# Order of the front: a weight block between row tiles of x, x turned by pairs, the bias row first

## The reference, cut to what matters

```
h = rmsnorm(x, g_mix)                      # x * rsqrt(mean(x*x) + EPS) * gain
proj = h @ w_in                            # 1024 x 6656
q, k, v, u, gate_a, gate_s = split(proj)   # u is 512 wide, the input of the SSM
attn = diff_attention(q, k, v, rel_bias[t5_bucket(rel)], ...)
y    = s5_ssm(u, ...)                      # parameters prepared from a_re, a_im, dt, b, c
mixed = sigmoid(gate_a)*attn + sigmoid(gate_s)*glu(gelu(y) @ w_glu)
x = x + mixed @ w_out;  x = x + relu(rmsnorm(x) @ w1)**2 @ w2;  return rmsnorm(x)
```

## Time and profile before

| | |
|---|---|
| median of 3 runs | 764.02 us (763.57 to 764.18) |
| profiled execution, its own time | 763.78 us |
| its span on the core | 762.0 us |
| PE busy | 745.2 us (98%), 3754 matmuls |
| DVE, ACT, POOL busy | 530.5, 359.2, 28.3 us |
| DMA | 85.21 MB, mean 112 GB/s |

### The profile page before, as it was taken

How to read it: one execution, slowest core, us unless ns; L and a number is a source line. 1 busy time by engine, 2 the same in 40 slices (tenths; PEclk the granted TensorE clock), 3 DMA queues, 4 the chain that set the end, 5 groups by cost and what they waited for, 6 DMA issues and landing times.

```text
span 762.0 us, 10030 instructions
## 1 busy us (share of the span) xinstructions
PE 745.2 (98%) x3754; PEld 608.7 (80%) x3754; DVE 530.5 (70%) x953; ACT 359.2 (47%) x630; POOL 28.3 (4%) x27
## 2 busy tenths in 40 slices
PE   5999999999999999999999999999999999999996
PEld 4878888777777777888888888788888888888885
DVE  4679999665556673436743578866886498748897
ACT  7524631265556663732322645434543345335455
POOL 3210000000000100000000000000000000000015
PEclk9999999999999999999999999999999999999998
DMA  7773439932224430237237130282108320742002
GB/s 246 203 163 116 103 110 163 209 93 71 70 70 122 155 111 3 87 106 248 83 111 194 57 109 29 65 225 98 56 1 235 124 84 0 186 146 83 28 1 111
DMA packets 91824, 85.21 MB, mean 112 GB/s; under 512 B 10028, under 2 KB 68064, under 8 KB 91776
## 3 DMA queue, kind: packets, MB, share of 16 engines
q1 hardware_dynamic: 90944, 82.85, 39.0%
q10 hardware_dynamic: 832, 1.71, 1.1%
HBM read 77.11 MB, written 5.34 MB: 108 GB/s over the span
## 4 chain that ended last, share of the span: by engine, by line
PE 90%; DVE 4%; ACT 3%; issue 2%; DMA 1%; POOL 0%; SPq 0%; DVEq 0%; ACTq 0%
PE ps L1651 27%; PE ps L1653 26%; PE ps L1652 26%; PE ps L1941 3%; PE ps L1922 2%; PE ps L1931 1%; DMA mixA<-in_x 1%; DVE w_lo L1414 1%; PE ps L1726 1%; DVE fr L1427 1%; ACT fa_hi L884 1%; PE ps L1855 1%; ACT w_hi L615 1%; PE ps L1838 1%; PE ps L1815 0%
## 5 line engine op out<-in xcount | busy, mean ns | idle before, releaser
L1651 PE MATMUL ps<-hT_hi,w_hi 128*128 128x512 f32 x384 | 152.5, 397 | 0.5 <-DVE hT_lo L983 0.3
L1653 PE MATMUL ps<-hT_hi,w_lo 128*128 128x512 f32 x384 | 149.9, 390 | 0.0
L1652 PE MATMUL ps<-hT_lo,w_hi 128*128 128x512 f32 x384 | 149.6, 390 | 0.0
L1651 PE MATMUL ps<-w_hi,hT_hi 128*128 128x512 f32 x288 | 113.9, 395 | 1.1 <-POOL w_lo L557 1.1
L1653 PE MATMUL ps<-w_hi,hT_lo 128*128 128x512 f32 x288 | 112.3, 390 | 0.0
L1652 PE MATMUL ps<-w_lo,hT_hi 128*128 128x512 f32 x288 | 112.1, 389 | 0.0
L851 ACT ACTIVATE w_hi<-raw 128x1024 fp32r<-128x1024 f32 x78 | 81.7, 1053 | 56.4 <-PE ps L1653 56.4
L1414 DVE TENSOR_TENSOR w_lo<-raw,w_hi 128x1024 fp32r<-128x1024 f32 x78 | 94.1, 1219 | 16.0 <-ACT w_hi L851 15.0
L615 ACT ACTIVATE w_hi<-raw 128x1024 fp32r<-128x1024 f32 x62 | 64.7, 1057 | 56.7 <-PE ps L1653 51.0
L1011 DVE TENSOR_TENSOR w_lo<-raw,w_hi 128x1024 fp32r<-128x1024 f32 x58 | 70.0, 1220 | 29.5 <-ACT w_hi L615 28.9
L1651 PE MATMUL ps<-w_hi,fa_hi 128*128 128x512 f32 x224 | 87.4, 390 | 1.0 <-DVE w_lo L1414 1.0
(11 more groups left out here) (258 smaller groups left out, 998.0 us busy)
## 6 DMA issues: line engine op xcount, KB each, us to landing
raw<-in_w SPq DMA_DIRECT2D x64, 512.0 KB, 4.2
raw<-in_w_in SPq DMA_DIRECT2D x44, 512.0 KB, 5.3
raw<-in_w_glu SPq DMA_DIRECT2D x8, 512.0 KB, 3.9
raw<-in_w_out SPq DMA_DIRECT2D x8, 512.0 KB, 3.9
mixA<-in_x SPq DMA_DIRECT2D x4, 512.0 KB, 5.1
bias<-frow_dram SPq DMA_DIRECT2D x32, 64.0 KB, 2.0
toep<-taps_dram SPq DMA_DIRECT2D x8, 256.0 KB, 12.5
x<-in_x SPq DMA_DIRECT2D x4, 512.0 KB, 6.7
```

The source lines that it names most:

```text
L1651: nc.tensor.matmul(dst, a_hi, b_hi, start=start, stop=False)
L1652: nc.tensor.matmul(dst, a_hi, b_lo, start=False, stop=False)
L1653: return nc.tensor.matmul(dst, a_lo, b_hi, start=False, stop=stop)
```

## The change

Three things are reordered; the arithmetic stays.

1. SP issues x tiles 0 and 1, unit 0, x tiles 2 and 3, units 1 to 3. `rb` and `oneh` move from SP's list to ACT's queue, behind the three gain columns, with a semaphore of their own (`onehot_in`).
2. x is turned and split by pairs. A pair g is the blocks k = 2g, 2g+1 of row tiles 0 and 1 (256 columns each); the "late" part is the same blocks of row tiles 2 and 3. For k = 0, 1 row tiles 2 and 3 are handled one by one (128 columns). The transposes stand partly between the products. `w_lo` of unit 0 is made by DVE in two halves; POOL makes units 1 to 3.
3. The two bias row matmuls are PE's first instructions, behind `onehot_in`; DVE's copies of `frow` stand between its scalings of row tiles 2 and 3.

```diff
 # SP
-        for u in range(RING):
+        load_x(0)
+        load_x(1)
+        load_raw(0)
+        load_x(2)
+        load_x(3)
+        for u in range(1, RING):
             load_raw(u)
...
-                         (rel_bias, rb[:, :]), (onehot, oneh[:, :]),
 # POOL
-        for u in range(U_V):
+        pool.wait_ge(w_lo_done, 1)
+        for u in range(1, U_V):
 # ACT
+        act.dma_start(rb[:, :], rel_bias).then_inc(onehot_in, 16)
+        act.dma_start(oneh[:, :], onehot).then_inc(onehot_in, 16)
...
+        x_stats(0)
+        x_stats(1)
         act.wait_ge(cols_turned, 1)
-        nc.scalar.activation(cols[:, :], ps[:, turn_bank(0, KT - 1), 0:2 * KT + UT],
-                             ACT.Identity).then_inc(cols_copied, 1)
+        nc.scalar.activation(cols[:, :], ps[:, 5, 0:2 * KT + UT], ACT.Identity).then_inc(cols_copied, 1)
...
+        def x_hi(k, t0, t1, done):
+            nc.scalar.activation(hT_hi[:, k, P * t0:P * t1], x_turned(k, t0, t1), ACT.Identity,
+                                 scale=g1_col[:, k:k + 1]).then_inc(done, 1)
+        def hi_pair(g):
+            act.wait_ge(pair_turned, g + 1)
+            for k in (2 * g, 2 * g + 1):
+                x_hi(k, 0, 2, pair_hi)
+        def hi_late(g):
+            act.wait_ge(turned, 2 * g + 2)
+            for k in (2 * g, 2 * g + 1):
+                x_hi(k, 2, 4, hT_hi_done)
         split_hi(0)
         act.wait_ge(cols_copied, 1)
-        for k in range(KT):
-            turn_hi(0, k, g1_col)
-            if k == 2:
-                split_hi(1)
+        hi_pair(0)
+        x_stats(2)
+        x_stats(3)
+        act.wait_ge(third_turned, 1)
+        for k in range(2):
+            x_hi(k, 2, 3, third_hi)
+        split_hi(1)
+        act.wait_ge(turned, 2)
+        for k in range(2):
+            x_hi(k, 3, 4, hT_hi_done)
+        hi_pair(1)
+        hi_late(1)
+        hi_pair(2)
+        hi_pair(3)
         for u in range(U_SSM, U_V):
             split_hi(u + 2)
             if u == 0:
+                hi_late(2)
+                hi_late(3)
                 act.wait_ge(prm_in, 16 * N_PRM)
 # DVE (x_lo, lo_pair, lo_late are the counterparts of x_hi, hi_pair, hi_late)
+        scale_x(0)
+        scale_x(1)
+        dve.wait_ge(w_hi_done, 1)
         dve.wait_ge(cols_copied, 1)
-        for k in range(KT):
-            turn_lo(0, k, g1_col)
+        TT(w_lo[:, 0, 0:512], raw[:, 0, 0:512], w_hi[:, 0, 0:512].bitcast(F32), ALU.subtract).then_inc(w0_part, 1)
+        lo_pair(0)
+        TT(w_lo[:, 0, 512:], raw[:, 0, 512:], w_hi[:, 0, 512:].bitcast(F32), ALU.subtract).then_inc(w_lo_done, 1)
+        scale_x(2)
+        dve.wait_ge(frow_mm, 1)
+        TS(frow[:, 0:512], ps[0:N_HEADS, 7, :], 1.0, None, ALU.mult).then_inc(frow_out, 1)
+        TS(frow[:, 512:BIAS_W], ps[0:N_HEADS, 6, 0:BIAS_W - 512], 0.0, MASKED, ALU.mult, ALU.add).then_inc(frow_out, 1)
+        scale_x(3)
+        dve.wait_ge(third_hi, 2)
+        for k in range(2):
+            x_lo(k, 2, 3, third_lo)
+        dve.wait_ge(hT_hi_done, 2)
+        for k in range(2):
+            x_lo(k, 3, 4, hT_lo_done)
+        lo_pair(1)
+        lo_late(1)
+        lo_pair(2)
+        lo_pair(3)
+        lo_late(2)
+        lo_late(3)
 # PE
+        pe.wait_ge(onehot_in, 32)
+        nc.tensor.matmul(ps[0:N_HEADS, 7, :], rb[:, :], oneh[:, 0:512], start=True, stop=True)
+        nc.tensor.matmul(ps[0:N_HEADS, 6, 0:BIAS_W - 512], rb[:, :], oneh[:, 512:BIAS_W], start=True,
+                         stop=True).then_inc(frow_mm, 1)
         pe.wait_ge(ident_set, 2)
+        pe.wait_ge(cols_in, 16 * N_COLS)
+        nc.tensor.transpose(ps[:, 5, 0:2 * KT + UT], cols_nat[:, :],
+                            ident[0:2 * KT + UT, 0:2 * KT + UT]).then_inc(cols_turned, 1)
+        pe.wait_ge(x_scaled, 1)
+        for k in range(4):
+            turn_x(0, k)
+        pe.wait_ge(x_scaled, 2)
+        for k in range(4):
+            mm = turn_x(1, k)
+            if k % 2:
+                mm.then_inc(pair_turned, 1)
+        def first_waits(t):
+            if t == 0:
+                pe.wait_ge(w0_part, 1)
+                pe.wait_ge(pair_lo, 1)
+            elif t == 1:
+                pe.wait_ge(cols_copied, 1)
+            elif t == 2:
+                pe.wait_ge(frow_out, 2)
+                pe.wait_ge(third_lo, 2)
+            else:
+                pe.wait_ge(hT_lo_done, 2)
         for u in range(U_SSM, U_V):
-            pe.wait_ge(w_lo_done, u + 1)
+            if u:
+                pe.wait_ge(w_lo_done, u + 1)
+                pe.wait_ge(pair_lo, 2 * u + 2)
             for t in range(TOK):
...
                 for k in (2 * u, 2 * u + 1):
+                    if u == U_SSM and t == 0 and k == 1:
+                        pe.wait_ge(w_lo_done, 1)
+                        pe.wait_ge(pair_lo, 2)
...
+                if u == U_SSM and t == 1:
+                    for t3 in range(2, TOK):
+                        pe.wait_ge(x_scaled, t3 + 1)
+                        for k3 in range(2):
+                            mm = turn_x(t3, k3)
+                        if t3 == 2:
+                            mm.then_inc(third_turned, 1)
+                        else:
+                            mm.then_inc(turned, 2)
+            if u == U_SSM:
+                turn_x_late(1)
+                turn_x_pair(2)
+                turn_x_pair(3)
+            if u == U_SSM + 1:
+                turn_x_late(2)
+                turn_x_late(3)
...
             row_unit_mm(u, (u - U_V) // 4, (u - U_V) % 4, 4, hT_hi, hT_lo, None, 0)
             if u == U_V:
                 turn_prm()
-                bias_row()
```

More of the change, by code:

```diff
@@ L214, in build @@
     c12_joined = sem("c12_joined"); p7_joined = sem("p7_joined"); c22_joined = sem("c22_joined"); c21_joined = sem("c21_joined")
-    consts_in = sem("consts_in"); prm_in = sem("prm_in"); gfin_in = sem("gfin_in")
+    consts_in = sem("consts_in"); onehot_in = sem("onehot_in"); w0_part = sem("w0_part"); prm_in = sem("prm_in"); gfin_in = sem("gfin_in")
     frow_out = sem("frow_out"); frow_done = sem("frow_done"); frow_mm = sem("frow_mm")
@@ L224, in build @@
     scale_ready = sem("scale_ready"); x_rt = sem("x_rt"); x_rstd = sem("x_rstd"); x_scaled = sem("x_scaled")
+    pair_turned = sem("pair_turned"); pair_hi = sem("pair_hi"); pair_lo = sem("pair_lo")
+    third_turned = sem("third_turned"); third_hi = sem("third_hi"); third_lo = sem("third_lo")
     turned = sem("turned"); hT_hi_done = sem("hT_hi_done"); hT_lo_done = sem("hT_lo_done")
@@ L378, in turn_bank, with x_place, x_turned @@
             return k - 4
-        return (B_T + k) % 8 if g == 0 else B_T + k % 4
+        return B_T + k % 4
+    def x_place(t, k):
+        c0 = 256 * (k % 2) + P * (t % 2)
+        bank = (2 if t == 2 else 3) if t >= 2 and k < 2 else ((0, 1, 2, 3), (None, 0, 1, 0))[t // 2][k // 2]
+        return bank, c0
+    def x_turned(k, t0, t1):
+        bank, c0 = x_place(t0, k)
+        return ps[:, bank, c0:c0 + P * (t1 - t0)]
     def wait_rows(eng, c, t):
@@ L390, in _, with load_x @@
     def _(sp):
-        for t in range(TOK):
+        def load_x(t):
             sp.dma_start(mixA[:, t, :], x[0, P * t:P * t + P, :]).then_inc(x_in[t], 16)
@@ L597, in _, with x_stats @@
             act.dma_start(dst, src).then_inc(cols_in, 16)
-        for t in range(TOK):
+        act.dma_start(rb[:, :], rel_bias).then_inc(onehot_in, 16)
+        act.dma_start(oneh[:, :], onehot).then_inc(onehot_in, 16)
+        def x_stats(t):
             act.wait_ge(x_in[t], 16)
@@ L985, in turn_lo, with scale_x @@
             ins.then_inc(hT_lo_done, 1)
-        for t in range(TOK):
+        def scale_x(t):
             dve.wait_ge(x_rt, t + 1)
@@ L992, in _, with x_lo, lo_pair, lo_late @@
             TS(mixA[:, t, :], mixA[:, t, :], rstd[:, 0, t:t + 1], None, ALU.mult).then_inc(x_scaled, 1)
-        dve.wait_ge(cols_copied, 1)
-        for k in range(KT):
-            turn_lo(0, k, g1_col)
+        def x_lo(k, t0, t1, done):
+            tc_ = slice(P * t0, P * t1)
+            STT(out=hT_lo[:, k, tc_], in0=x_turned(k, t0, t1), scalar=g1_col[:, k:k + 1],
+                in1=hT_hi[:, k, tc_].bitcast(F32), op0=ALU.mult, op1=ALU.subtract).then_inc(done, 1)
+        def lo_pair(g):
+            dve.wait_ge(pair_hi, 2 * g + 2)
+            for k in (2 * g, 2 * g + 1):
+                x_lo(k, 0, 2, pair_lo)
+        def lo_late(g):
+            dve.wait_ge(hT_hi_done, 2 * g + 2)
+            for k in (2 * g, 2 * g + 1):
+                x_lo(k, 2, 4, hT_lo_done)
+        scale_x(0)
+        scale_x(1)
+        dve.wait_ge(w_hi_done, 1)
+        dve.wait_ge(cols_copied, 1)
+        TT(w_lo[:, 0, 0:512], raw[:, 0, 0:512], w_hi[:, 0, 0:512].bitcast(F32), ALU.subtract).then_inc(w0_part, 1)
[18 more added lines that the diff above has]
+        lo_late(3)
         def prow(i):
@@ L1730, in turn_x @@
         def turn_x(t, k):
-            return nc.tensor.transpose(ps[:, turn_bank(0, k), P * t:P * t + P], mixA[:, t, P * k:P * k + P],
```

(18 more changed lines are left out.)

17 lines of the change are left out of this document (8 added, 9 removed).

## The result

| | before | after |
|---|---|---|
| median of the runs | 764.1 us (763.57 to 767.92) | 781.56 us (780.62 to 782.6) |
| ratio | | 1.0223 (1.0212 to 1.0234) |
| profiled execution | 763.78 us | 782.6 us |
| its span | 762.0 us | 780.8 us |

The change makes the kernel 17.5 us slower, against a forecast of 6.3 with an upper bound of 8.2. The sign was right and the size far out.

The account below looks back on a forecast made before the run. PE's matmul stream, busy 98% of the span, was taken as the bound, its shift carried to the end. 2.8 + 1.3 + 0.9 + 2.5 - 1.2 = +6.3 on 764.0 gave 770.3 us, range 766.0 to 772.2.

Parts of the forecast that it names:

- Steps 1 and 2: Front: one-hot table lands at 9.6 us, bias row takes 2.2, first product starts at 14.7 against 14.17.
- Step 3: Unit 0: waits on DVE and ACT before row tiles 2 and 3 end it at 22.5, not 19.74: +2.8 us.
- Steps 4 to 6: Transposes inside the stream +1.3 and +0.9, hole before unit 3 +2.5, bias row leaving after unit 4 -1.2 us.
- step 5: Unit 3: its split waits behind ACT's list, so PE has a hole; +2.5 us, bounds 2.3 and 3.2.
- The last paragraph: Signs to check in the trace, among them unit 4 starting near 43.4 and PE idling 2.3 to 3.2 before unit 3.
- the clock falls in the hole: Rival: PE's clock drops in the hole before unit 3, some 3.7 us at half speed lose 1.8: 772.1; chance 0.10.
- nothing behind it waits for a fixed time: Behind unit 4: every microsecond its start moves is carried unchanged to the end.
- nothing more is late: Behind the hole before unit 3: splits and low parts of later units still come in time, no further loss.
- at nothing: Changes counted as free: SP's order, its shorter list, POOL without unit 0, later frees of the raw ring.
- step 7: SP's reordered loads, its shorter list, POOL's lost unit 0 and later raw ring frees add no further time.
- step 6: Behind unit 4: the bias row leaves the stream, -1.2 us; DVE loses frow copies that PE did not wait for.
- The other side: Rival at the front: oneh lands by 5, first product at 9.8, unit 0 ends at 15.7: 763.5; chance 0.13.

Follow-up runs that it names:

- the exponentials first: Changed kernel, ACT making the exponentials and unit 3's split before the late parts of pairs 2 and 3, DVE's late parts also later: 778.19 us, ratio 1.0176.
- the bias row back: Changed kernel with the bias row matmuls and DVE's frow copies behind unit 4 again, rb and oneh staying on ACT's queue: 771.33 us, ratio 1.0083.
- matmuls through the gap: Changed kernel with bias row and ACT order edits, warm-up and row tile 2 turned early, plus 12 fp32 matmuls behind the first pair's turning: 764.5 us.
- held store: Changed kernel with one more ACT wait, putting the frow store 0.4 us behind the last load of u: 782.2 us, ratio 1.0184.
- DVE's wait: Changed kernel with the frow store held behind the loads of u, and DVE's large products waiting for GpSimd's copy: 774.21 us, ratio 1.013.
- the late store: Changed kernel with ACT's store of the bias rows moved to one unit behind the turning of u: 771.75 us, ratio 1.0128.

## Why the prediction was right in sign and wrong in size

- **Steps 1 and 2 held.** The table landed at 9.0 (9.6; the range was made for 9.0 to 10.7), the bias row took 2.2, the first product came at 14.64 (14.7). ACT's wait for the turned columns was 4.7 us, as said.
- **Step 3 was mis-sized**, +4.9 and not +2.8. I priced the products of unit 0 at 0.23 each, and twelve of them took 0.43. I had noted that the clock goes from 1.2 to 2.4 GHz at 10.3 in the kernel before, and took that as a time of day. It is none: it rose at 4.93 where PE worked from 1.5 on, at 20.0 in the kernel after, whose PE starts at 9.05 and not 6.67 and is idle in between, and once at 14.92 behind the same transposes as before. With the clock the order of waits changed too. I had DVE as the last before row tile 2, at 18.9; it was free at 18.0 and waited 3.0 us more for the transposes, which PE reached at 19.9. The wait before row tile 3 did not come.
- **Steps 4 to 6 held.** Transposes inside the stream, the hole of 2.2 and 0.3 of lost overlap before unit 3 (+2.5), the bias row (-1.15). L1025's counterpart took 0.28 us, as step 5 assumed. (The last paragraph has unit 4 near 43.4; its own terms give 43.6.) The run with the exponentials first shows that the hole is made by ACT's order.
- **The rival "the clock falls in the hole" happened** in the profiled run, with the price it had (1.7 for 1.8), and I gave it 0.10. I had argued from a fall 2.6 us after the last matmul of the program that a hole of 2.5 was just too short; the hole was 2.2, and the fall came all the same. It is a matter of the run: the six times of the kernel after lie in two groups, 780.62 to 780.82 and 782.29 to 782.6, 1.7 apart, which is what one such fall costs. The trace is of the second group; that the first ran without the fall is not shown.
- **Where it failed: "nothing behind it waits for a fixed time", and with it "nothing more is late" in step 5 and "at nothing" in step 7.** I took a stream without a hole up to unit 4 to be one that carries a shift unchanged to the end. It has a second chain beside it, from u through memory and GpSimd back to PE, and that one was not shifted but reordered. In step 6 I saw that DVE is rid of the `frow` copies and that PE did not wait for them; I did not ask who else waited. ACT did, with the store of 640 KB, and its wait was what kept the store behind the loads of u. Then the copy missed its place ahead of DVE's products. It cost 8.7 of the 12.5 us by which the forecast was short of the profiled run; late clock in unit 0 and clock behind the hole are the rest (2.1 and 1.7). The store is not the whole of it: with the store behind the loads, but the clock down behind the hole, the time was 782.2. The shift of u against DVE's block (13.0 against 7.8 us), which I had taken for one and the same, is enough for the same 8.7.
- The other side, an early front, stayed out because of the table, as argued. But the run with the bias row back shows that it would not have won even so: with the exponentials first as well and first products at 10.5 to 11.4, three of the four kernels end 1.4 to 3.5 us behind the old one (764.57 in the runs beside them), and the one with matmuls through the gap is level with it (764.5, ratio 0.9999 to 1.0016).

## What to carry to other kernels

When an operation moves to an earlier place, follow everything that waited for its result, the DMAs first: a wait that costs nothing may be what keeps a large store behind a load that matters. A shift of the main stream may be added up only as far as the next place where a second chain (memory, another engine) joins it, and each such place has to be looked up with its slack on both sides. Price matmuls behind a changed start at both clock levels, and count a hole like the one of 2.2 us here as a hole plus a possible 1.7 us of slow matmuls. Before a difference of a microsecond or two between medians is put down to an edit, look in the traces for where it lies.

## What the runs showed of the hardware that was not expected

- A GpSimd copy of 128 x 2048 took 1.9 us beside an idle DVE or ahead of its work, and 15.6 us when it came 0.6 us behind the start of DVE's back-to-back operations with two SBUF inputs. A start 2.8 us earlier (58.51, bias row back) against 61.35 (held store) is worth 13.5 us of the copy and the hole of 6.4 at PE. It goes the other way too: in the kernel before the copy came first, at 49.19, and the DVE operation of 49.25 (two SBUF inputs, 128x32) took 1.88 us, where its twin in the kernel after took 0.19.
- A store of 640 KB out of 8 partitions had at most 8 packets under way for 13 us and stretched a load of 512 KB issued behind it from 6.6 to 19.2 us; issued 0.4 us behind the load, it did not (6.6).
- The granted clock came down for 3.4 us after PE idles of 2.2 to 2.7 us, though not after each one: 2.2 us before unit 3 was followed by a fall in the profiled runs of the kernel after, the bias row back, the held store and DVE's wait, and by none with the late store. Warm-up ahead of such an idle stretch was worth 0.3 us at unit 4; matmuls through it were worth 1.4 us (765.94 to 764.5).
- The column of the granted clock reads 1.00 at the front of these traces, up to the clock's first record, also where matmuls step by 0.43. There the level has to be read from the step of the matmuls.
